# First stage of a two-block transformer kernel: TensorE sums the squares of x, the first loads and activation tables come in another order, and the first weight unit is split in four

## The chip, the cores and the metric

The kernel runs on one core of one Trainium2 chip. The metric is the device time of one execution in microseconds (us). It has five instruction streams: TensorE (PE in the rows, with its weight loads as PEld), VectorE (DVE), ScalarE (ACT), GpSimd (POOL) and SyncE (SP), which issues nearly all DMA transfers. A PE row with `f32` is fp32 or fp32r data of 4 bytes.

## The reference

x has 256 tokens of 1024 channels. The first block computes `h = rmsnorm(x, norm_mix_g)` and `p = h @ w_in`, and goes on from p to a sliding-window attention and an mLSTM, an output projection, a cross attention to `mem` and a feed-forward layer; a second block follows (gated delta rule, then stick-breaking attention). What matters here is the very first step:

```
def rmsnorm(x, g):
    y = x * rsqrt(mean(x * x, axis=-1) + 1e-6)
    return y * g
p = rmsnorm(x, norm_mix_g) @ w_in        # 1024 x 2824
```

Beside it `c_act = silu(c_2)`, a vector of 1024, is computed at the start and used by the second block's modulation matrices.

## The kernel before, in words

**Layout.** x lies transposed in SBUF: 8 chunks of 128 channels on the partitions, 256 tokens in the free dimension. It is loaded in four transfers x0 to x3 of two chunks each (256 KB). A weight matrix is cut into units of 1024 x 256 (1 MB); a unit is loaded into one of NRAW = 5 buffers `raw`, and split into two fp32r tiles: `whi` (a ScalarE copy, job `hi`) and `wlo = raw - whi` (VectorE, job `lo`), each in PIECES = 4 pieces of two chunks. A product of the two activations tiles `p0hi`, `p0lo` with them is three fp32r matmuls of 128x256 per 128 columns (line 1841), so a unit is 48 matmuls in four parts of 12.

**The order of work** is written by a planner, class `Plan`: it makes one list of jobs, and each engine runs its own jobs of this list in that order, waiting on semaphores. LAG = 1 means that the `lo` of a piece is put behind the `hi` of the next one. Nothing is reordered when the kernel runs.

**The first stage.** ScalarE waits for the vector table `vec` (192 KB, with gains and c), computes silu(c) (line 999), then squares each x pair (job `sq`, line 1032) into one of two buffers `tr`. VectorE adds the two halves and adds up the pairs (job `sqadd`, lines 1399 to 1404) into `acc`. TensorE multiplies `acc` with a matrix of ones in plain fp32 (job `ones`, line 1870), which sums over the partitions and leaves the sum in every row of PSUM bank `stats`. ScalarE loads the table set with ln and exp (line 994) and computes rs = exp(-0.5 ln(sum/1024 + eps)) (job `rs`, lines 1046 and 1048; it also waits for `con`, the first 264 columns of constants with the ones matrix and eps). Then the job list has the four `hi` pieces of the first weight unit with three of its `lo`, then the norm in five groups of 1, 1, 2, 2, 2 chunks (GROUPS): `xg` is x*gain*rs on VectorE (one instruction per chunk, line 1373), `ghi` the fp32r copy on ScalarE (line 1061), `glo` the remainder on VectorE (line 1376). Then `cr` (a constant, line 1445), and the products of the first unit, between which the pieces of the next unit are split.

**The DMA queue of SP** issues, in this order: vec, x0 to x3, con, weight units 0 to 2, conr, the rest of con, the two gate matrices g, units 3 and 4, mem; from unit 5 on it waits until the buffer's last `lo` is done.

`arrived(k)` is what a reader of unit k waits for: the semaphore of its buffer, which each load raises by 16. `stats_free()` makes TensorE wait until the last user of the bank `stats` has read it.

Of the kernel before, what the change touches and what calls it, by code (L numbers as in the profile page):

```python
# [14 lines left out]
T = 256  # L15
# [6 lines left out]
NRAW = 5  # L22
# [3 lines left out]
PIECES = 4  # L26
# [24 lines left out]
NCON0 = 8 + 2 * 128  # L51
# [97 lines left out]
def is_ada(unit):  # L149
# [4 lines left out]
COUNTED = {  # L154
    "hi": "hi", "lo": "lo", "unit": "unit", "adarow": "adarow", "adacp": "adacp", "adacol": "adacol",
    "adaadd": "adaadd",
    "sq": "sq", "sqadd": "sqadd", "ones": "ones", "rs": "rs",
    "xg": "norm_dve", "xm": "norm_dve", "xs": "norm_dve", "glo": "norm_dve", "fin": "norm_dve",
    "xa": "norm_act", "ghi": "norm_act",
    "aq": "proj_act", "ak": "proj_act", "cid": "proj_act", "csilu": "proj_act", "mo": "proj_act",  # L160
# [31 lines left out]
class Plan:  # L192
# [17 lines left out]
    def add(self, kind, *i):  # L210
        self.jobs.append((kind, *i))
        self.done.add((kind, *i))
# [158 lines left out]
    def make(self):  # L371
        add = self.add
        later = self.deferred.append
        add("csilu", "c")
        for i in range(4):
            self.stat("mix", i)
        self.rstd("mix")
        self.load_units()
        for _ in range(PIECES):
            self.prep_unit()  # L380
        for _ in self.gain_steps("mix"):
            pass
        add("cr")

        def on_mqk(i):
# [374 lines left out]
def program(nc, xT, memT, vec, con, conr, wg1, wg2, wst, wsd, outT):  # L760
# [11 lines left out]
    with ctx:  # L772
# [3 lines left out]
        def sem(name):  # L776
            return ctx.enter_context(nc.semaphore(name))

        S = {n: sem("s_" + n) for n in sorted(set(COUNTED.values()))}
        s_raw = [sem(f"s_raw{i}") for i in range(NRAW)]  # L780
        s_in = {n: sem("s_in_" + n) for n in ("x0", "x1", "x2", "x3", "mem", "vec", "con", "con2", "conr", "g")}
        s_out = sem("s_out")
# [2 lines left out]
        def on(*job):  # L785
            return S[COUNTED[job[0]]], rank[job]

        def tick(kind):
            return S[COUNTED[kind]], 1

        def landed(name):
            return s_in[name], 32 if name == "g" else 16

        def arrived(k):
            return s_raw[k % NRAW], 16 * (k // NRAW + 1)

        def at(name, i=0):
            return plan.at(name, i)
# [5 lines left out]
        raw = [sb(f"raw{i}", [P, 2048]) for i in range(NRAW)]  # L804
        whi = [sb(f"whi{i}", [P, 2048], F32R) for i in range(NHL)]
        wlo = [sb(f"wlo{i}", [P, 2048], F32R) for i in range(NHL)]
        cst = sb("cst", [P, NCON])
        crt = sb("crt", [P, NCONR], F32R)
        vc = sb("vc", [P, NVEC])
        x = sb("x", [P, KC, T])  # L810
# [12 lines left out]
        rs = sb("rs", [P, T])  # L823
# [43 lines left out]
        def V(name, i=0, n=1, p=P):  # L867
            a = VEC[name][0]
            return vc[0:p, a + i:a + i + n]
# [9 lines left out]
        ident, ones = C("ident"), C("ones")  # L879
# [56 lines left out]
        def sq_tile(site, i):  # L936
            if site == "mem":
                return flat(xk[:, 2 * i:2 * i + 2, :])
            return tr[4 + i % 2]

        stats = ps[7]
# [6 lines left out]
        @block.sync  # L948
        def _(e):
            def load(name, dst, src):  # L950
                e.dma_start(dst, src).then_inc(s_in[name], 16)

            na = nb = 0
            load("vec", vc[:, :], vec)
            for i in range(4):
                load(f"x{i}", x[:, 2 * i:2 * i + 2, :], xT[:, 2 * i:2 * i + 2, :])
            load("con", cst[:, 0:NCON0], con[:, 0:NCON0])
            for k, (name, i, kc, w) in enumerate(units):
                if k == 3:
                    load("conr", crf, conr)  # L960
                    load("con2", cst[:, NCON0:], con[:, NCON0:])
                    load("g", g1[:, :, :], wg1)
                    load("g", g2[:, :, :], wg2)
                if k == 5:
                    load("mem", m_x[:, :, :], memT)
                if kc == 8:
                    src = wst[na]
                    na += 1
                else:
                    src = wsd[nb]  # L970
                    nb += 1
                if k >= NRAW:
                    if is_ada(units[k - NRAW]):
                        e.wait_ge(*on("adarow", k - NRAW))
                    else:
                        e.wait_ge(*on("lo", k - NRAW, 3))
                e.dma_start(raw[k % NRAW][:, 0:kc * w], src).then_inc(s_raw[k % NRAW], 16)
            for i in range(4):
                e.wait_ge(*on("resb", i))
                e.dma_start(outT[:, 2 * i:2 * i + 2, :], x[:, 2 * i:2 * i + 2, :]).then_inc(s_out, 16)  # L980
            e.wait_ge(s_out, 64)
# [6 lines left out]
        def _(act):  # L988
            e, own = Once(act), Own(own_act)
# [7 lines left out]
            def silu(out, in_, f=ACT.Silu):  # L997
                table["lnexp"] = False
                return act.activation(out, in_, f)

            e.wait_ge(*landed("vec"))
            e.wait_ge(zeroed, 1)
            silu(cact[:, :, 0], V("c", 0, 8)).then_inc(*tick("csilu"))
            for kind, *i in jobs:
                if kind == "hi":
                    k, q = i
                    kc, w = units[k][2:]
                    per = -(-kc // PIECES)
                    a, b = q * per * w, min(kc, (q + 1) * per) * w
                    n = real[k] - 1  # L1010
                    e.wait_ge(*arrived(k))
                    if n >= NHL:
                        e.wait_ge(S["unit"], n - NHL + 1)
                    act.activation(whi[n % NHL][:, a:b], raw[k % NRAW][:, a:b], ACT.Copy).then_inc(*tick("hi"))  # L1014
                elif kind == "adacp":
                    k, = i
                    e.wait_ge(*on("adarow", k))
                    act.activation(arow[:, :], stats[:, T:2 * T], ACT.Copy).then_inc(*tick("adacp"))
                elif kind == "sq":
                    site, n = i  # L1020
# [6 lines left out]
                    else:  # L1027
                        e.wait_ge(*on("res", {"x": "wout", "ffn": "xo", "kv": "outa"}[site], n))
                    if n >= 2:
                        e.wait_ge(*on("sqadd", site, n - 2))  # L1030
                    src = NORM[site][0]
                    act.activation(sq_tile(site, n), flat(src[:, 2 * n:2 * n + 2, :]), ACT.Square).then_inc(*tick("sq"))  # L1032
                elif kind == "rs":
                    site, = i
                    e.wait_ge(*on("ones", site))
                    e.wait_ge(*landed("con"))
                    if site == "x":
                        e.wait_ge(*on("xg", "mem", 4))
# [10 lines left out]
                elif kind == "ghi":  # L1049
                    site, n = i  # L1050
# [11 lines left out]
                elif kind == "xa":  # L1062
                    site, n = i
# [3 lines left out]
                    for c in range(*GROUPS[n]):  # L1067
                        ins = act.activation(tmp[:, c, :], tmp[:, c, :], ACT.Identity, scale=mod[:, A + c:A + c + 1],  # L1068
                                             bias=mod[:, B + c:B + c + 1])
# [3 lines left out]
                elif kind == "aq":  # L1073
                    n, = i
# [5 lines left out]
                elif kind == "cid":  # L1080
                    n, = i
                    bank = bank_of("mqk", n)
                    e.wait_ge(*unit_done("mqk", n))
                    for m in range(2):
                        c = 2 * n + m
                        ins = act.activation(mqk[:, c, :], bank[:, m * T:(m + 1) * T], ACT.Identity,
                                             scale=V("cqk_w", c * 4 + 3), bias=V("cqk_b", c))
                    ins.then_inc(*tick("cid"))
                elif kind == "csilu" and i != ["c"]:
                    n, = i  # L1090
# [278 lines left out]
        def _(v):  # L1369
# [8 lines left out]
            for kind, *i in jobs:  # L1378
# [13 lines left out]
                elif kind == "sqadd":  # L1392
# [1 line left out]
                    s = sq_tile(site, n)  # L1394
                    e.wait_ge(*on("sq", site, n))
                    if n == 0:
                        if site != "mix":
                            e.wait_ge(*on("ones", {"mem": "mix", "x": "mem", "ffn": "x", "kv": "ffn"}[site]))
                        v.tensor_tensor(acc[:, :], s[:, 0:T], s[:, T:2 * T], ALU.add).then_inc(*tick("sqadd"))
                    else:  # L1400
                        own.mark(v.tensor_tensor(s[:, 0:T], s[:, 0:T], s[:, T:2 * T], ALU.add))
                        e.wait_ge(*own.last)
                        e.wait_ge(*on("sqadd", site, n - 1))
                        v.tensor_tensor(acc[:, :], acc[:, :], s[:, 0:T], ALU.add).then_inc(*tick("sqadd"))
# [398 lines left out]
        def _(t):  # L1803
# [8 lines left out]
            for kind, *i in jobs:  # L1812
# [51 lines left out]
                elif kind == "ones":  # L1864
# [3 lines left out]
                    stats_free()  # L1868
                    stat.append(("rs", site))
                    t.matmul(stats[:, 0:T], ones, acc[:, :], start=True, stop=True).then_inc(*tick("ones"))  # L1870
                elif kind == "f_ones":
                    e.wait_ge(*on("dacc", 7))
                    t.matmul(ps[3], ones, acc2[:, :], start=True, stop=True).then_inc(*tick("f_ones"))
# [375 lines left out]
```

## Time and profile before

| | |
|---|---|
| median of 3 runs | 995.97 us (995.44 to 1001.0) |
| the profiled execution | 992.34 us, of which span 990.6 us |
| TensorE busy (matmul) | 908.5 us, 92% of the span |
| VectorE, ScalarE busy | 601.1 us, 504.4 us |
| mean granted TensorE clock | 0.962 |
| moved by DMA | 148.25 MB, mean 150 GB/s |

The times in the rows are counted from the span's start. The profile was taken of one execution; its time is 3.6 us under the median of the others. TensorE's clock has two levels here, 2.4 GHz (a granted clock of 1.00) and 1.2 GHz (0.50). The chain of waits is the path that ended last, followed back from the last instruction; in its rows "issue" is time in which the engine waited for nothing that the profile shows.

### The profile page before, as it was taken

The numbers are of one execution on the slowest core, as the hardware profiler recorded it, in microseconds if no ns is written. First come the engines' busy times: TensorE is split into PE (matmuls) and PEld (weight loads), VectorE is DVE, ScalarE is ACT, GpSimd is POOL, SyncE is SP. The second block draws the span as 40 slices with busy tenths as digits, with TensorE's granted clock in tenths as the row PEclk, the third lists the DMA queues.
The fourth block names the chain that finished last, engine by engine and source line by source line (L and its number), as shares of the span: only waits on it lengthen the run. The fifth ranks groups of instructions, "written<-read, shape, count | busy, mean of one in ns | idle before, by whom it ended". The sixth has DMA issues, their size and how long they took to land.

```text
span 990.6 us, 16996 instructions
## 1 busy us (share of the span) xinstructions
PE 908.5 (92%) x7132; PEld 837.2 (85%) x7132; DVE 601.1 (61%) x1215; ACT 504.4 (51%) x1029; POOL 0.5 (0%) x5
## 2 busy tenths in 40 slices
PE   3979899999999999999969899989898879999998
PEld 3957698989899999999959687979797778988888
DVE  5378756675577777775656576666665465443345
ACT  5245554444445555555564625352644457456762
POOL 0000000000000000000000000000000000000000
PEclk9898999999999999999977899999999979999999
DMA  9423444563356676655652423223222134642211
GB/s 347 148 73 119 143 171 164 207 219 128 118 183 216 250 255 239 229 179 190 208 191 98 152 97 135 74 85 129 85 86 85 43 128 138 247 169 86 69 61 43
DMA packets 22541, 148.25 MB, mean 150 GB/s; under 512 B 2625, under 2 KB 3137, under 8 KB 6337
## 3 DMA queue, kind: packets, MB, share of 16 engines
q1 hardware_dynamic: 22464, 147.17, 41.6%
q8 instruction: 56, 0.92, 0.4%
q14 instruction: 21, 0.16, 0.0%
HBM read 146.11 MB, written 1.05 MB: 149 GB/s over the span
## 4 chain that ended last, share of the span: by engine, by line
PE 80%; DVE 11%; ACT 7%; issue 1%; DMA 1%; SPq 0%; DVEq 0%; ACTq 0%
PE ps L1841 55%; PE ps L1854 3%; PE ps L2073 2%; PE ps L2066 2%; DVE wlo L1376 2%; PE ps L2058 2%; PE ps L1884 1%; DVE kT L1373 1%; PE ps L1862 1%; ACT L994 1%; PE ps L2140 1%; DVE vt L1373 1%; ACT tmp L1068 1%; PE ps L2131 1%; PE ps L2004 1%
## 5 line engine op out<-in xcount | busy, mean ns | idle before, releaser
L1841 PE MATMUL ps<-p0hi,whi 128*128 128x256 f32 x1128 | 338.5, 300 | 16.9 <-DVE p0lo L1376 12.4
L1841 PE MATMUL ps<-p0lo,whi 128*128 128x256 f32 x1128 | 324.5, 288 | 0.0
L1841 PE MATMUL ps<-p0hi,wlo 128*128 128x256 f32 x1128 | 324.2, 287 | 0.0
L1376 DVE TENSOR_TENSOR wlo<-raw,whi 128x512 fp32r<-128x512 f32 (+2 forms) x436 | 272.8, 659 | 17.2 <-ACT whi L1014 15.4
L1841 PEld LDWEIGHTS ps<-p0hi,whi 128*128 128x128 f32 x1128 | 221.6, 196 | 34.4 <-issue 24.9
L1014 ACT ACTIVATE whi<-raw 128x512 fp32r<-128x512 f32 (+2 forms) x436 | 239.8, 600 | 8.3 <-DMA raw<-wst 8.2
L1841 PEld LDWEIGHTS ps<-p0lo,whi 128*128 128x128 f32 x1128 | 222.1, 197 | 0.7 <-issue 0.5
L1841 PEld LDWEIGHTS ps<-p0hi,wlo 128*128 128x128 f32 x1128 | 221.5, 196 | 0.0
L1841 PE MATMUL ps<-zhi,whi 128*128 128x256 f32 x176 | 49.3, 280 | 0.0
L1841 PE MATMUL ps<-zlo,whi 128*128 128x256 f32 x176 | 49.1, 279 | 0.0
L1841 PE MATMUL ps<-zhi,wlo 128*128 128x256 f32 x176 | 49.1, 279 | 0.0
L1841 PE MATMUL ps<-q1hi,whi 128*128 128x256 f32 x128 | 39.4, 308 | 3.3 <-DVE q1lo L1376 3.3
L1841 PE MATMUL ps<-q1lo,whi 128*128 128x256 f32 x128 | 37.6, 294 | 0.0
L1841 PE MATMUL ps<-q1hi,wlo 128*128 128x256 f32 x128 | 37.4, 292 | 0.0
L1854 PE MATMUL ps<-raw,cact 128*32 128x256 f32 x512 | 36.3, 404 | 0.0
L1391 DVE TENSOR_TENSOR mod<-ps,vc 128x2 f32<-128x2 f32 x32 | 5.0, 156 | 48.9 <-PE ps L1862 48.9
L1841 PEld LDWEIGHTS ps<-zhi,whi 128*128 128x128 f32 x176 | 33.1, 188 | 0.4 <-DVE tr L1511 0.4
L1841 PEld LDWEIGHTS ps<-zlo,whi 128*128 128x128 f32 x176 | 33.1, 188 | 0.0
L1841 PEld LDWEIGHTS ps<-zhi,wlo 128*128 128x128 f32 x176 | 33.1, 188 | 0.0
L1733 DVE TENSOR_TENSOR tmp<-ps,cst 128x512 f32<-128x512 f32 x24 | 16.5, 688 | 27.1 <-PE ps L2058 27.0
L1373 DVE SCALAR_TENSOR_TENSOR tr<-ps,tr 128x384 f32<-128x384 f32 (+1 forms) x21 | 11.6, 551 | 33.4 <-ACT tr L1356 29.0
L1032 ACT ACTIVATE tr<-x 128x512 f32<-128x512 f32 x16 | 10.1, 632 | 42.1 <-DVE x L1497 28.0
(338 smaller groups left out, 1589.6 us busy)
## 6 DMA issues: line engine op xcount, KB each, us to landing
raw<-wst SPq DMA_DIRECT2D x125, 1024.0 KB, 5.0
raw<-wsd SPq DMA_DIRECT2D x16, 704.0 KB, 4.8
x<-xT SPq DMA_DIRECT2D x4, 256.0 KB, 4.9
m_x<-memT SPq DMA_DIRECT2D x1, 1024.0 KB, 18.1
outT<-x SPq DMA_DIRECT2D x4, 256.0 KB, 2.3
cst<-con SPq DMA_DIRECT2D x1, 768.0 KB, 13.2
smo<-conr SPq DMA_DIRECT2D x1, 192.0 KB, 11.8
vc<-vec SPq DMA_DIRECT2D x1, 187.5 KB, 2.4
```

The source lines that it names most:

```text
L994: act.preload_act_table_set(LNEXP)
L1014: act.activation(whi[n % NHL][:, a:b], raw[k % NRAW][:, a:b], ACT.Copy).then_inc(*tick("hi"))
L1032: act.activation(sq_tile(site, n), flat(src[:, 2 * n:2 * n + 2, :]), ACT.Square).then_inc(*tick("sq"))
L1068: ins = act.activation(tmp[:, c, :], tmp[:, c, :], ACT.Identity, scale=mod[:, A + c:A + c + 1], bias=mod[:, B + c:B + c + 1])
L1373: return v.scalar_tensor_tensor(out=out, in0=a, scalar=s, in1=b, op0=op0, op1=op1)
L1376: return v.tensor_tensor(lo, src, hi.bitcast(F32), ALU.subtract)
L1733: v.tensor_tensor(Xm[n_ % 2][:, :, :], ps[4 + 2 * (n_ % 2)].rearrange("p (n t) -> p n t", n=4), rep(C("mlev", lev * P, (lev + 1) * P), 4), ...
L1841: ins = t.matmul(o, a, b, start=first and q == 0, stop=last and q == len(ops) - 1, skip_group_check=True)
L1854: ins = t.matmul(stats[g:g + 32, T:2 * T], cact[:, c, :], r[:, c * T:(c + 1) * T], start=c < 4, stop=c >= 4)
L2058: ins = t.matmul(ps[4 + 2 * (n_ % 2)][:, n * P:(n + 1) * P], Am[n_ % 2][:, n // 2, n % 2 * P:(n % 2 + 1) * P], Tm[n_ % 2][:, n, :], start= ...
L2066: ins = t.matmul(ps[4 + 2 * (n_ % 2)][:, n * P:(n + 1) * P], Um[n_ % 2][:, n, :], Xm[n_ % 2][:, n, :], start=True, stop=True)
L2073: ins = t.matmul(ps[3 + 2 * (n_ % 2)][:, n * P:(n + 1) * P], Xm[n_ % 2][:, n, :], Um[n_ % 2][:, n, :], start=True, stop=True)
```

## The change

Four things are changed, all of them before the first product:

- The sum of squares. The four `sqadd` and the `ones` of this norm are gone. In their place TensorE takes each squared pair as it comes (job `mones`): two plain fp32 matmuls of 128x256 with the ones matrix, eight in all, which add up in `stats`. A square buffer is now freed by the `mones` that read it. The other norms keep the old way.
- The first loads. `con` and `vec`, in this order, are issued by ScalarE's queue at its start and no longer by SP's. SP begins with x0.
- The tables. The ln/exp table set is loaded right behind silu(c), ahead of the first square.
- The first weight unit. It is loaded in four quarters of 512 columns (256 KB, rows of 2 KB), each with a semaphore of its own. Its `hi` and `lo` pieces no longer stand ahead of the norm but one each behind the norm's groups 1 to 4. The planner therefore gives VectorE this order: xg0, xg1, glo0, xg2, glo1, xg3, glo2, lo piece 0, xg4, glo3, lo piece 1, glo4, lo piece 2, cr, lo piece 3; before, lo pieces 0 to 2 stood in front of xg0 and lo piece 3 behind cr.

```diff
@@ class Plan, make
         add("csilu", "c")
         for i in range(4):
-            self.stat("mix", i)
-        self.rstd("mix")
+            add("sq", "mix", i)
+            add("mones", i)
+        add("rs", "mix")
         self.load_units()
-        for _ in range(PIECES):
-            self.prep_unit()
-        for _ in self.gain_steps("mix"):
-            pass
+        for step, _ in enumerate(self.gain_steps("mix")):
+            if step in (1, 2, 3, 4):
+                self.prep_unit()
         add("cr")
@@ arrived
-            return s_raw[k % NRAW], 16 * (k // NRAW + 1)
+            return s_raw[k % NRAW], 16 * (k // NRAW + (k % NRAW > 0))
@@ SP
             na = nb = 0
-            load("vec", vc[:, :], vec)
             for i in range(4):
                 load(f"x{i}", x[:, 2 * i:2 * i + 2, :], xT[:, 2 * i:2 * i + 2, :])
-            load("con", cst[:, 0:NCON0], con[:, 0:NCON0])
...
-                e.dma_start(raw[k % NRAW][:, 0:kc * w], src).then_inc(s_raw[k % NRAW], 16)
+                if k == 0:
+                    for q in range(4):
+                        e.dma_start(raw[0][:, q * 512:(q + 1) * 512], src[:, q * 512:(q + 1) * 512]).then_inc(s_first[q], 16)
+                else:
+                    e.dma_start(raw[k % NRAW][:, 0:kc * w], src).then_inc(s_raw[k % NRAW], 16)
@@ ScalarE
+            act.dma_start(cst[:, 0:NCON0], con[:, 0:NCON0]).then_inc(s_in["con"], 16)
+            act.dma_start(vc[:, :], vec).then_inc(s_in["vec"], 16)
             e.wait_ge(*landed("vec"))
             e.wait_ge(zeroed, 1)
             silu(cact[:, :, 0], V("c", 0, 8)).then_inc(*tick("csilu"))
+            lnexp()
...
-                    e.wait_ge(*arrived(k))
+                    if k:
+                        e.wait_ge(*arrived(k))
+                    else:
+                        e.wait_ge(s_first[q], 16)
...
                     if n >= 2:
-                        e.wait_ge(*on("sqadd", site, n - 2))
+                        e.wait_ge(*(on("mones", n - 2) if site == "mix" else on("sqadd", site, n - 2)))
...
-                    e.wait_ge(*on("ones", site))
+                    e.wait_ge(*(on("mones", 3) if site == "mix" else on("ones", site)))
@@ TensorE
+                elif kind == "mones":
+                    n, = i
+                    e.wait_ge(*on("sq", "mix", n))
+                    e.wait_ge(*landed("con"))
+                    for c in range(2):
+                        ins = t.matmul(stats[:, 0:T], ones, sq_tile("mix", n)[:, c * T:(c + 1) * T], start=n + c == 0, stop=n + c == 4)
+                    ins.then_inc(*tick("mones"))
+                    if n == 3:
+                        stat.append(("rs", "mix"))
```

## Rows read from the trace of the kernel before

**Rows 1.** The page, part 4, shares of the chain that ended last.

```profile
PE 80%; DVE 11%; ACT 7%; issue 1%; DMA 1%; SPq 0%; DVEq 0%; ACTq 0%
```

**Rows 2.** Chain of waits, 0 to 20 us: start us, us, what.

```profile
2.57 6.19 DMA x<-xT
8.78 0.64 ACT tr L1032
9.44 0.44 DVE tr L1401
9.90 0.44 DVE acc L1404
10.38 1.23 PE ps L1870 x2
11.63 1.28 ACT L994
12.92 0.48 ACT rs L1046
13.43 0.42 ACT rs L1048
...
17.74 2.26 PE ps L1841 x9
```

**Rows 3.** Timeline of VectorE: start us, us, operation, idle before it.

```profile
14.40 1.89 DVE L1376 TENSOR_TENSOR wlo<-raw,whi 128x512 fp32r<-128x512 f32 x3 [4.07 <-ACT whi L1014]
16.21 0.87 DVE L1373 SCALAR_TENSOR_TENSOR tmp<-x,vc,rs 128x256 f32<-128x256 f32 x2
...
20.03 0.87 DVE L1373 SCALAR_TENSOR_TENSOR tmp<-x,vc,rs 128x256 f32<-128x256 f32 x2
```

**Rows 4.** Timeline of the queue of SP and of ScalarE at the start.

```profile
0.73 0.37 SPq L951 DMA_DIRECT2D vc<-vec  x1
...
1.12 1.28 ACT L999 ACT_TABLE_LOAD   x1 [1.12 <-POOL cact L985]
3.15 0.22 ACT L999 ACTIVATE cact<-vc 128x8 f32<-128x8 f32 x1 [0.75 <-DMA vc<-vec]
```

**Rows 5.** DMA issues of the first 60 us: KB each, median us from issue to landing.

```profile
cst<-con SPq DMA_DIRECT2D x1, 132.0 KB, 6.1
vc<-vec SPq DMA_DIRECT2D x1, 187.5 KB, 2.4
```

**Rows 6.** Stretches of 5 and 1 us: busy per engine; last columns PEclk, DMA share, GB/s.

```profile
0.00:5.00 5.00, 0.00 (x0) 0.00 (x0) 0.00 (x0) 1.50 (x2) 0.51 (x5) 1.00 0.48 140
5.00:6.00 1.00, 0.00 (x0) 0.00 (x0) 0.15 (x1) 0.78 (x2) 0.00 (x0) 1.00 0.89 270
```

**Rows 7.** Line 1870 from 10 to 12.5 us: duration ns min/median/max, start us, form.

```profile
L1870 PE MATMUL ps<-acc,cst x2: 634/714/793, 10.4 to 11.0; 128*128 128x256 f32 x2
```

**Rows 8.** Eight fp32 matmul records of 128x256 in the chain of waits.

```profile
250.25 1.73 PE ps L1985 x8
```

**Rows 9.** Timeline of TensorE where the spacing of the first unit's products changes.

```profile
21.72 0.38 PE L1841 MATMUL ps<-p0hi,whi 128*128 128x256 f32 x1
...
21.93 0.28 PE L1841 MATMUL ps<-p0lo,whi 128*128 128x256 f32 x1
...
22.05 0.28 PE L1841 MATMUL ps<-p0hi,wlo 128*128 128x256 f32 x1
```

**Rows 10.** Split of the first weight pieces, VectorE: duration ns min/median/max.

```profile
L1376 DVE TENSOR_TENSOR wlo<-raw,whi x8: 682/684/691, 14.4 to 24.9; 128x512 fp32r<-128x512 f32 x8
```

**Rows 11.** Stretches of 1 us behind a gap of TensorE, columns as in rows 6.

```profile
220.00:221.00 1.00, 0.00 (x0) 0.00 (x0) 0.91 (x2) 1.00 (x3) 0.00 (x0) 1.00 0.00 0
...
223.00:224.00 1.00, 1.00 (x8) 1.00 (x8) 1.00 (x3) 1.00 (x3) 0.00 (x0) 0.65 0.00 0
...
226.00:227.00 1.00, 1.00 (x8) 1.00 (x7) 0.64 (x2) 0.00 (x0) 0.00 (x0) 0.64 0.85 352
```

**Rows 12.** The longest piece of the chain of waits from 10 to 50 us.

```profile
17.74 21.76 PE ps L1841 x168
```

More of the change, by code:

```diff
@@ L156 @@
     "adaadd": "adaadd",
-    "sq": "sq", "sqadd": "sqadd", "ones": "ones", "rs": "rs",
+    "sq": "sq", "sqadd": "sqadd", "ones": "ones", "mones": "ones", "rs": "rs",
     "xg": "norm_dve", "xm": "norm_dve", "xs": "norm_dve", "glo": "norm_dve", "fin": "norm_dve",
@@ L779, in program @@
         S = {n: sem("s_" + n) for n in sorted(set(COUNTED.values()))}
+        s_first = [sem(f"s_first{q}") for q in range(4)]
         s_raw = [sem(f"s_raw{i}") for i in range(NRAW)]
@@ L1396, in _ @@
                     if n == 0:
-                        if site != "mix":
-                            e.wait_ge(*on("ones", {"mem": "mix", "x": "mem", "ffn": "x", "kv": "ffn"}[site]))
+                        if site != "mem":
+                            e.wait_ge(*on("ones", {"x": "mem", "ffn": "x", "kv": "ffn"}[site]))
                         v.tensor_tensor(acc[:, :], s[:, 0:T], s[:, T:2 * T], ALU.add).then_inc(*tick("sqadd"))
```

## Prediction, on record before the change was run

> **What bounds the kernel now.** I read the page first: four fifths of the chain that ended last are TensorE work [rows 1], so time is won only where TensorE stands still or runs at its low clock. Then the chain at the start, because the whole change lies ahead of the first product. It shows a latency chain [rows 2]: the last pair x3 lands at 8.76 (2.57 + 6.19), its square ends at 9.42, two adds, the ones matmul to 11.61, the table load of 1.28, Ln and Exp until 13.85, and the first product only at 17.74. From there 168 product records follow without a gap to 39.50 [rows 12]: the first units are fed well enough once they have begun. So the change is worth, in first order, the distance by which 17.74 moves. The timeline of VectorE shows why rs at 13.85 does not yet start the norm: three weight pieces stand in front, and xg0 begins at 16.21 [rows 3]. From xg0 to the product are 17.74 - 16.21 = 1.53.
>
> The sum is made against the profiled execution, 992.34 us. The median of the three runs is 995.97, 3.6 above it; I add my difference to that median.
>
> **The change, part by part.**
>
> *Loads.* SP's first issue took 0.37 and the next came 0.43 later (0.73 to 1.16 in the same timeline; the first start is in [rows 4]). Without vec in front, x0 to x3 go out 0.43 earlier. But con (132 KB) now competes with x instead of following it: at the 270 GB/s of the stretch from 5 to 6 [rows 6] it costs x3 some 0.5. x3 then lands at about 8.76 - 0.43 + 0.5 = 8.8, unchanged. Three more issues on SP for the quarters delay units 1 and 2 by about 1.3, three times 0.43; no one waits for them: unit 0 is not wanted before its first `hi`, which comes after rs, and unit 1 only after unit 0's four pieces. I cost the quarters at nothing; the cover is the whole chain to rs.
>
> *vec.* Here it turns. vec was first and landed 2.4 after its issue [rows 5]; silu(c) ran at 3.15, long before x0 [rows 4]. Now it is the second transfer of another queue. Bounds: 2.4 after an issue at about 1.2, so 3.6, if the second queue has a free way; con's 6.1 [rows 5] after 1.2, so 7.3, if it fares as the transfer that stood behind x. In between: con, vec and the half of x that is served beside them are 0.83 MB. Before, 0.70 MB were moved by 5.0 (140 GB/s over 5 us) and 0.83 by 5.5 [rows 6]; 0.43 earlier is 5.1, and 0.5 from the last byte to the semaphore (vec before: 192 KB moved, landed at 3.13) makes 5.6. I take **5.6**, with 3.6 and 7.3 as ends.
>
> *Tables.* Before, silu's table load ran at 1.12 while vec was on its way. The second load, 1.28 [rows 2], leaves the place between the ones matmul and Ln and stands between silu (0.22, [rows 4]) and the first square. With vec at 5.6: silu to 5.84, load to 7.13, first square to 7.78. Before, the first square ended at about 5.8. Its saving of 1.28 at the end is real only if TensorE is not the one that comes last.
>
> The trace shows a load of 1.28 with Ln 0.01 behind it [rows 2]. The Trainium skill ("ScalarE: Activation LUTs", What ACT_TABLE_LOAD costs) counts about 1.38 more for a drain with each switch of sets. The rows here show no such piece; by the page the first square would end 1.4 later, and my result would be 998.9.
>
> *TensorE sums the squares.* This is the costly part. Before, one fp32 matmul of 256 columns: two records, 793 and 634 ns, 1.23 together [rows 7, 2]; the second began 0.43 after the first (11.60 - 0.79 = 10.81 against 10.38). At the high level eight records took 1.73 [rows 8], 0.216 each, so a matmul is 0.43 at the high level and 0.85 at the low one, plus 0.37 after the last one is streamed (1.23 - 0.85). Eight matmuls are **6.8 at the low level**, 3.5 at the high one. TensorE has done nothing before, and begins at the low level: the first unit's products are spaced 0.21 until 21.93 and 0.12 after it [rows 9], although the page's column says 1.00; the rise came 4.2 after the first product. In its place went seven adds of VectorE, of which two (0.92) were on the path.
>
> So first matmul at 7.83, rise 4.2 later at 12.0; by then 4.2 of 6.8 are done, the other 2.6 take 1.3 at the high level, and with 0.3 behind the last the sum stands at **13.6**. The squares of x2 and x3 wait for the matmuls of x0 and x1 (two buffers), but TensorE always has the next pair by then; it is TensorE that comes last, not x3: 8.8 + 0.63 + one pair (1.71 + 0.37) would be 11.5. Before, Ln began at 12.92; now at 13.65. rs at 13.65 + 0.93 = 14.58 (12.92 to 13.85 before), **0.7 later**.
>
> *Norm and weight pieces.* xg0 follows rs at once, at 14.6: this wins 16.21 - 13.85 = 2.36. But the first product now needs lo piece 0, and that stands behind xg0, xg1, glo0, xg2, glo1, xg3, glo2 in VectorE's order. Before, xg0 to the end of glo2 went from 16.21 to 20.03 [rows 3], 3.82; with lo piece 0, 0.68 [rows 10], and 0.14 to the product it is 4.64 instead of 1.53, **3.11 lost**. Net of this part: 0.75 lost. ScalarE's pieces fit between its norm copies and are not last. First product: 14.58 + 0.03 + 4.64 = **19.2**, against 17.74: **1.5 later**.
>
> *After it.* The rest of VectorE's work was only reordered. Behind lo piece 0 come 0.87 + 0.69 + 0.68, so part 1 has its piece 2.2 after the first product; part 0 takes 12 x 0.214 = 2.6 at the low level. No wait, and a margin of 0.4. TensorE has idled 5.6 since the ones and begins low again, as before. All that follows is shifted.
>
> Sum: +0.7 + 0.8 = +1.5: 992.34 + 1.5 = 993.8 for a profile, and 995.97 + 1.5 = **997.5** for the median. This is no change by measurement: about 1% (10 us) can be told from none.
>
> **Rivals.**
>
> *A, TensorE is not last.* vec lands at 3.6 (first square ends at 5.8, as before) and the clock rises after 3 us. Then 3.0 of 6.8 are done at 8.9, the rest would end at 10.8, and x3's pair binds: 9.4 + 0.05 + 0.85 + 0.3 = 10.6. Either way about 10.8; Ln at 10.85, rs 11.8, first product 16.5: **-1.3, 994.7**. For it: ScalarE's queue is empty. Against it: the DMA engines' share was 0.89 in the stretch from 5 to 6 [rows 6]. The Trainium skill ("DMA: Bandwidth & Descriptors", Issuing engines are not separate DMA queues) speaks against this rival and against the change: transfers issued by several engines share the same 16 DMA engines, and only issue time is saved. Chance 0.2.
>
> *B, slower than forecast.* vec lands at 7.3 and the clock does not rise in the sum: first matmul at 9.5, sum at 9.5 + 6.8 + 0.4 = 16.7, rs 17.7, first product 22.3: **+4.6, 1000.6**. It decides from a vec later than about 6.5. Chance 0.15.
>
> *C, the clock outlives the gap.* The eight matmuls raise the clock and the products start high. Then a unit is bound by VectorE instead: 2.2 for part 0, then three parts of 1.44, 6.5 against 19 x 0.214 + 29 x 0.12 = 7.5 before: 1.0 back, **+0.5, 996.5**. Against it: TensorE stood 2.13 at 220 and the clock fell at 223.3, rising again near 226.6, though it worked from 222 on [rows 11]; here the gap is 5.6. The Trainium skill ("TensorE: Matmul & The Clock Gate", HAM oscillation) says the same of gaps between bursts. Chance 0.1.
>
> *D, clearly slower.* A shift of a few us moves later stretches against the falls of the clock. A fall as at 223.3 to 226.6 [rows 11] costs half its 3.3, 1.7; it takes six more of them for 10 us, **1006**. Place: the late stages with gaps on TensorE. Chance 0.03; the mirror image, **986**, 0.02.
>
> That the change does nothing at all is one more case: quarters and SP order surely do nothing, but the sum on TensorE cannot be idle.
>
> **How the numbers follow.** Forecast (+0.3 to +3) 0.5; A 0.2, B 0.15, C 0.1, D and its mirror 0.05. Predicted 997.5. The range reaches from A with a margin of 1.5 for the scatter of runs (995.44 to 1001.0 before), 993.2, to B, 1000.8. A, B, C and the forecast all lie within 1%: same 0.95, slower 0.03, faster 0.02.
>
> **What would show it.** Right: eight fp32 matmuls (16 records) ending near 13.6, table load between silu and the first square at about 6, the first square after 7, xg0 right behind Exp, a product near 19.2 spaced 0.21 at first, nothing of the quarters in any wait. Wrong: the sum ending before 11 (A), after 15.5 (B), the first products spaced 0.12 (C), or a first product near the old time with a total that differs by more than 3 us, which then comes from elsewhere.

## The result, and the profile after

The changed kernel takes 1004.17 us (median of 7 executions, 996.65 to 1004.83), the kernel before, beside it, 995.44 (7 executions, 988.89 to 1001.0). The ratio is 1.0085, 95% interval 1.0045 to 1.0126: slower. The forecast was 997.5 and its range ended at 1000.8. The difference is under 1%, but its interval does not reach 1.

Two more series, on two chips, gave 1.0071 (1.0044 to 1.0097) and 1.0026 (0.9998 to 1.0055), with means 4.9 and 3.1 above the kernel before beside them. Ahead of the first of the two I had expected 3 to 4 if only the delay of the first product is lasting, and 7 to 9 if something of the change makes the clock fall more often; it came between. Over all 31 executions of the change the mean is 1001.2, over 116 of the kernel before 995.9: the lasting loss is **5.3 us**, smaller than the first median says. (Errors given here and below are standard errors of the difference of two means; this one is 0.7.)

One execution of the kernel before at 1077.1, with a granted clock of 0.794, is a slow run and left out everywhere, while four of the 116, at 1002.5 to 1003.3, are also over 1.5% above their fastest but have the clock of their neighbours (0.949 to 0.951) and are kept: without them the loss is 5.6.

The profiled execution took 1004.83, with a span of 1003.0 against 990.6.

Below, the head is the time from the start to the first product. The chain of waits of the changed kernel from 0 to 22 us (start us, us, what), to be read beside [rows 2]:

```profile
1.17 5.74 DMA vc<-vec
...
6.94 0.22 ACT cact L1002
...
7.17 1.28 ACT L997
...
8.46 0.64 ACT tr L1041
...
9.15 6.15 PE ps L1885 x16
...
15.32 0.48 ACT rs L1055
...
15.83 0.42 ACT rs L1057
...
16.28 0.49 DVE tmp L1382
...
19.59 0.60 DVE p0lo L1385
20.19 0.61 DVE wlo L1385
...
20.85 1.22 PE ps L1850 x4
```

The chain no longer begins with x but with vec, which lands at 6.91. Then silu, the table load and one square follow each other, and the sixteen records of the sum (line 1885; two records for each of the eight matmuls) take 6.15 until 15.30. rs is ready 2.4 later than before (16.25 against 13.85), and the norm begins at once behind it. From xg0 to the first product are 4.57, against 1.53 before. The first product comes at 20.85, **3.1 later** than the 17.74 of before.

The two transfers of ScalarE's queue, from the DMA issues of the first 4 us (KB each, us to landing), against 6.1 and 2.4 in [rows 5]:

```profile
vc<-vec ACTq DMA_DIRECT2D x1, 187.5 KB, 5.7
cst<-con ACTq DMA_DIRECT2D x1, 132.0 KB, 4.1
```

The head is 3.1 of the 12.4 us by which the spans differ. Where the rest is, three stretches tell. First the kernel before, then the changed one (busy per engine, then PEclk, DMA share, GB/s):

```profile
550.00:580.00 30.00, 25.94 (x176) 22.19 (x175) 15.54 (x32) 16.74 (x36) 0.00 (x0) 0.89 0.34 133
...
700.00:730.00 30.00, 27.12 (x207) 24.25 (x204) 19.23 (x37) 16.67 (x32) 0.00 (x0) 1.00 0.29 106
...
770.00:800.00 30.00, 26.88 (x202) 25.75 (x203) 17.79 (x34) 13.36 (x25) 0.00 (x0) 0.94 0.23 75
```

```profile
550.00:580.00 30.00, 25.68 (x149) 20.24 (x142) 15.78 (x33) 15.53 (x32) 0.00 (x0) 0.77 0.38 141
...
700.00:730.00 30.00, 27.30 (x188) 23.58 (x187) 16.17 (x30) 19.26 (x35) 0.00 (x0) 0.90 0.27 95
...
770.00:800.00 30.00, 24.61 (x140) 21.49 (x139) 12.49 (x24) 11.15 (x21) 0.00 (x0) 0.72 0.10 36
```

Nearly the same work (in the second trace it stands 3 to 13 us later) meets more of the low clock: 0.77, 0.90 and 0.72 instead of 0.89, 1.00 and 0.94. With VectorE's instructions of both traces matched by form and order, the changed kernel is 3.2 behind at 40 us, 4.4 from 110, 2.9 from 230 to 550, 6.0 from 560, 9.1 from 720 and 12.8 from 780. Each step is a stretch in which the clock stands low in one profile and high in the other. The one step back, 1.5 at 223, is the fall at 223.3 to 226.7 that the kernel before has [rows 11] and the changed one has not. Nothing there was edited. The mean granted clock is 0.947 against 0.962, which is 106 us at the low level against 75 (twice the missing share, times the span).

### The profile page after: what moved, and what is told of

Its sections match the earlier page's. It is cut to its first block, busy times and chain, and to the rows that moved or that the text cites. A ratio compares the mean times of both kernels' runs of the same rounds, so it can differ in the third digit from the quotient of the medians.

```text
span 1003.0 us, 17016 instructions
## 1 busy us (share of the span) xinstructions
PE 921.4 (92%) x7146; PEld 848.0 (85%) x7146; DVE 598.4 (60%) x1208; ACT 504.4 (50%) x1029; POOL 0.5 (0%) x5
## 4 chain that ended last, share of the span: by engine, by line
PE 79%; DVE 11%; ACT 7%; issue 1%; DMA 1%; ACTq 0%; DVEq 0%
PE ps L1850 54%; PE ps L1863 3%; PE ps L2091 2%; PE ps L2084 2%; PE ps L2076 2%; DVE wlo L1385 2%; PE ps L1902 1%; PE ps L1871 1%; DVE kT L1382 1%; ACT L997 1%; PE ps L2158 1%; DVE vt L1382 1%; ACT tmp L1077 1%; PE ps L2149 1%; PE ps L2022 1%
## 5 line engine op out<-in xcount | busy, mean ns | idle before, releaser
L1385 DVE TENSOR_TENSOR wlo<-raw,whi 128x512 fp32r<-128x512 f32 (+2 forms) x436 | 273.2, 660 | 14.2 <-ACT whi L1023 12.5
```

Source lines behind the costliest of these rows:

```text
L1385: return v.tensor_tensor(lo, src, hi.bitcast(F32), ALU.subtract)
```

## The experiments

**The stand of the clock.** By this I mean where the rises and falls of the clock lie against the work. For each profile I read when the clock first falls after the first product. In the kernel before that is within the gate matmuls, 32 of 8 columns each (line 1884), which run from 39.50 to 43.46. In the kernel before and then in the changed one:

```profile
42.00:43.00 1.00, 1.00 (x9) 1.00 (x8) 0.00 (x0) 0.00 (x0) 0.00 (x0) 0.70 0.00 0
```

```profile
44.00:45.00 1.00, 1.00 (x10) 1.00 (x10) 0.00 (x0) 0.00 (x0) 0.00 (x0) 0.90 0.07 16
```

A mean of 0.70 over 1 us at levels of 1.00 and 0.50 puts the fall at 42.40, that is 24.66 after the first product (17.74); a mean of 0.90 puts it at 44.80, 23.95 after 20.85. The table has this distance for every profile, and the rest of the span behind the first product:

| first fall less first product | rest of the span | profile of |
|---|---|---|
| 23.35, 23.43, 23.47, 23.60, 23.69 | 975.0, 974.8, 975.1, 975.3, 975.1 | early matmuls, delay ahead, pieces first, change again, best |
| 23.95, 24.08 | 982.1, 982.5 | the change (above, and beside the delays) |
| 24.23, 24.23, 24.23, 24.35 | 982.3, 975.5, 975.6, 975.6 | delay behind (twice), vec before con, VectorE sum |
| 24.66, 24.82, 24.85 | 972.9, 972.7, 972.8 | before, best with whole unit, before + delay |
| 25.04 | 976.8 | before + early table |
| 26.40, 26.47 | 974.3, 977.8 | vec first, change + longer delay |

Kernels that differ in the edits below, with nearly the same distance, agree within 0.5 us (first row) and 0.2 (fourth), and one kernel at two distances (the change) differs by 7. So what follows the head is the same work in all of them, and its time goes with where the clock's changes stand against it. The first fall alone does not settle it: at 24.23 one kernel, the delay behind, has both 982.3 and 975.5, and the two of the last row, 0.07 apart, differ by 3.5. These may be edges between two courses of the clock; nothing here tested that. The stand differs from execution to execution, and with it the time of the unchanged kernel, 987.4 to 1003.3.

**Early TensorE work alone**, on no path: the kernel before with

```diff
+            e.wait_ge(*landed("x0"))
+            for _ in range(5):
+                t.matmul(ps[6][:, 0:T], x[:, 0, 0:P], x[:, 1, :], start=True, stop=True)
```

> The kernel before, with five plain fp32 matmuls of 128x256 on x0 that no one reads, on TensorE from 5.2 to about 9.5, ahead of the ones matmul. They are on no path. Theory: time and first product (17.7) as before, within 1 us in the mean. Rival (early work of TensorE changes where or how often the clock falls later): mean 3 us or more above before, with more stretches at the low clock in the trace.

First product at 17.57, mean of 12 executions 995.9 beside 995.7 of before; ratio 1.0009 (0.9984 to 1.0034). The matmuls from 4.81 to 9.44 cost nothing that can be told from zero. The test is weaker than it looks: their ten records took 4.63, as the low level gives for ten (0.43 each, and 0.37 behind the last), and the trace records no rise before 20.45. So it says that early work at the low clock is not the cause; it does not test early work that raises the clock, as the sum does.

**A pure delay** in the kernel before, ahead of its last addition of the squares:

```diff
+                        if site == "mix" and n == 3:
+                            for _ in range(4):
+                                own.mark(v.tensor_tensor(flat(tmp[:, 0:2, :]), s[:, :], s[:, :], ALU.add))
+                                e.wait_ge(*own.last)
```

> The kernel before, with four additions of 128x512 that no one needs on VectorE ahead of the last addition of the squares: a pure delay of 2.9 us on the chain, first product near 20.6, nothing else changed. Theory (the loss behind the head is only the stand of the later stages against the clock's falls, which are tied to the program's start): the total is 8 to 9 us above before, like the change. Rival (the falls of the clock stand differently in every execution, so a shift costs itself alone): 2.9 above before, 998.5, with the scatter of before.

First product at 20.53; ratio 1.0029 (0.9997 to 1.0061), mean 997.8 against 995.8: the delay of 2.8 costs 2.0 with an error of 1.3. A shift nearly as large as the change's costs itself, as far as that error tells. The theory, that any shift would cost 8 to 9, is refuted; the falls are not tied to the program's start: the first stood at 45.38 instead of 42.40, 24.85 behind the product instead of 24.66.

**vec first**, con alone on ScalarE's queue:

```diff
+            load("vec", vc[:, :], vec)
             for i in range(4):
                 load(f"x{i}", ...)
...
-            act.dma_start(vc[:, :], vec).then_inc(s_in["vec"], 16)
```

> The change, with vec back at the head of SP's queue and con alone on ScalarE's. Theory (vec's landing starts the late sum, TensorE's eight matmuls bound it): vec lands near 3.2, first square ends near 5.9 on x0, the eight fp32 matmuls end near 12.0, first product near 17.6 instead of 20.85. Rival (the eight matmuls are the cost whatever starts them, or con is late): sum ends after 14, first product after 19.5. For the total: if the loss behind the head (5.6 of 8.7 us) comes from where the later stages stand against the falls of the clock, it goes with the head and the total is that of before within 2 us; if the loss is from something else that the change leaves in the kernel, 1000 or more remain.

Its chain from 0 to 22 us:

```profile
0.73 2.89 DMA vc<-vec
...
5.86 5.57 PE ps L1885 x16
...
16.98 5.06 PE ps L1850 x22
```

vec lands at 3.62, the sum begins 3.3 earlier than in the change and still takes 5.57, and the first product comes at 16.98, 3.9 earlier than in the change and 0.8 earlier than before. The head is as expected; the total is not: ratio 1.0026 (0.9998 to 1.0054), mean 998.9 against 995.8. That is neither the total of before within 2 nor the 1000 or more of the rival: a head better than before's goes with a total 3.1 above it, with an error of 1.2.

**The sum on VectorE** as before, loads, tables and pieces of the change (the diff shows the order of jobs; the waits go with it):

```diff
-            add("sq", "mix", i)
-            add("mones", i)
-        add("rs", "mix")
+            self.stat("mix", i)
+        self.rstd("mix")
```

> The change, with the squares summed on VectorE and one ones matmul as before; loads, tables and weight pieces as in the change. Theory: vec still lands near 6.9, squares end near 10.8, adds 0.9, matmul 1.23, rs near 13.9, first product near 18.5, that is 2.3 earlier than the change and 0.8 later than before. Rival (vec alone is the cost): first product stays above 20. Rival on the clock: the eight early matmuls are what puts the later falls of the clock elsewhere; then the total falls by clearly more than 2.3.

```profile
1.18 5.44 DMA vc<-vec
...
11.45 0.44 DVE acc L1412
...
11.93 1.24 PE ps L1878 x2
...
13.19 0.48 ACT rs L1054
...
18.71 3.36 PE ps L1849 x14
```

The sum ends at 13.17 though vec is late (6.62), 2.1 ahead of the sum on TensorE, or 1.8 if the 0.3 by which vec was earlier is taken off. Ratio 1.0023 (0.9995 to 1.005), mean 998.1: 2.3 above before, with an error of 1.3, for a first product 1.0 later.

**The four pieces ahead of the norm**, as before, the rest of the change:

```diff
-        for step, _ in enumerate(self.gain_steps("mix")):
-            if step in (1, 2, 3, 4):
-                self.prep_unit()
+        for _ in range(PIECES):
+            self.prep_unit()
+        for _ in self.gain_steps("mix"):
+            pass
```

> The change, with the four weight pieces ahead of the norm as before; sum on TensorE, loads and tables as in the change. Theory: rs stays at 16.25, first product 3.9 behind it near 20.15, 0.7 earlier than the change: the interleaving itself loses 0.7. Rival (the interleaving gains, as it lets the norm start 2.4 earlier): first product 21.5 or later. Total: 0.7 less than the change if the clock's falls stay where they are; up to 6 less if a shift of 0.7 brings the later stages elsewhere against them.

```profile
8.92 5.35 PE ps L1886 x16
...
17.66 0.41 DVE tmp L1383
...
19.11 2.90 PE ps L1851 x12
```

rs was ready at 15.21, the first product 3.90 behind it; in the change it was 4.60 behind. So the interleaving loses 0.70. Ratio 1.0034 (1.001 to 1.0059), mean 999.3: 3.4 above before, with an error of 1.0, for a first product 1.4 later.

**The table load alone**, in the kernel before: `lnexp()` behind silu(c).

> The kernel before, with the ln/exp table loaded right behind silu(c); nothing else changed. Theory: the load ends near 4.7, before x0 is there, so it is hidden; Ln starts 1.28 earlier near 11.65 and the first product comes near 16.5; mean of the total 1.3 under before. Rival by the Trainium skill (ScalarE: Activation LUTs, What ACT_TABLE_LOAD costs, with about 1.38 of drain at each switch): the first square would start near 6.1 instead of 5.2, and a gap would stand behind the load.

```profile
10.46 1.24 PE ps L1871 x2
11.72 0.48 ACT rs L1047
...
16.54 3.54 PE ps L1842 x15
```

Ln follows the ones matmul at once; the first product is 1.2 earlier and the mean 993.7 against 995.7 (ratio 0.998, 0.9954 to 1.0006). Of the 1.38 of drain that the Trainium skill names (ScalarE: Activation LUTs, What ACT_TABLE_LOAD costs) no run here shows anything: in the change silu begins at 6.94 for 0.22, the load at 7.17, the square at 8.46.

**vec before con**, both on ScalarE's queue, the rest of the change:

> The change, with vec issued ahead of con on ScalarE's queue. Theory (vec is late because con's transfer stands in front of it and x's packets are served beside it): vec lands between 3.5 and 4.8 instead of 6.0 to 6.9, con between 4.5 and 6.5, and the sum begins at 6.3 or so, first product near 17.9. Rival (a transfer on ScalarE's queue is slow in itself beside SP's): vec lands after 5.5.

```profile
0.73 4.13 DMA vc<-vec
...
7.10 6.43 PE ps L1885 x16
...
19.07 5.98 PE ps L1850 x34
```

vec lands at 4.86: con in front of it made 1.2 to 2.0 of its lateness. Another 1.2 go when vec stands at the head of SP's queue, ahead of x (3.62); whether x beside it or ScalarE's queue made these, no run here separates. The first product is later than expected because the sum began at 7.1, not 6.3, and took 6.43. The one execution took 996.51.

**Does the sum on TensorE tie the first product to the clock?** The change, vec first and pieces first, all with the sum on TensorE, had totals above what their heads explain, by 2.6, 3.9 and 2.1. The sum's length goes with the clock's rise in it: 5.32 to 6.43 in ten profiles. In the trace the rise is seen in the weight loads of the sum (shortest, median and longest in ns; the change, then the delay behind): 338 at the low level, 190 at the high one, and more of them short where the rise comes early.

```profile
L1885 PEld LDWEIGHTS ps<-tr,cst x16: 190/338/338, 9.1 to 14.7; 128*128 128x128 f32 x16
```

```profile
L1889 PEld LDWEIGHTS ps<-tr,cst x16: 186/229/337, 8.4 to 13.1; 128*128 128x128 f32 x16
```

The clock's record in the trace begins with this rise, at 14.07 in the change, 4.9 behind the start of the sum; over the ten profiles it comes 2.9 (sum 5.32) to 5.5 (sum 6.43) behind the start. A rise that is 2.6 later ends the sum 1.1 later. So the first product follows the rise: it came 6.5 to 7.7 behind it in the seven profiles without a delay between. The theory is that its distance to the clock's later changes therefore takes only a part of the values that it takes in the kernel before. In the table six of these seven stand at 23.43 to 24.23 and one at 26.40, none with a rest under 974.3; of the seven profiles without that sum five stand at 24.35 to 25.04, three of them with the best rest, 972.7 to 972.9. Delays test it. In the change, between rs and xg0 (1.9 us, and with two more additions 3.4):

```diff
+                    if site == "mix" and n == 0:
+                        for w in (2, 2, 1):
+                            own.mark(v.tensor_tensor(flat(tmp[:, 0:w, :]), flat(x[:, 0:w, :]), flat(x[:, 0:w, :]), ALU.add))
+                            e.wait_ge(*own.last)
```

> The change, with three additions that no one needs on VectorE between rs and xg0: a pure delay of 1.9 us ahead of the first product. Theory: the sum on TensorE ends sooner or later with the moment at which the clock rises in it, so it ties the first product to the clock's changes, and ties it where the later stages meet more falls; a delay behind the sum moves the product off that place. Then the mean falls in spite of the delay, from the change's 1001.5 (19 executions) to 997 to 999, with executions under 995, which the change does not have. Rival (the excess of 3 us over the head is the change's own in some other way, or is chance): the delay adds itself, mean 1003.4.

> The change, with five such additions, a delay of 3.4 us. Theory: the first product stands against the clock's changes as in the change again, so the mean is the change's plus 3.4, near 1005, some 6 to 8 above the kernel with the delay of 1.9 though only 1.5 more was put in. Rival: 1.5 above that kernel.

With 1.9: ratio 1.0059 (1.0038 to 1.0081), mean of 8 executions 999.3. With 3.4: 1.0111 (1.0078 to 1.0143), mean of 6 executions 1004.7. The second is 5.4 above the first for 1.5 more delay, with an error of 1.5 (6 to 8 expected). The executions under 995 that I expected of the first did not come (lowest 996.61), and before was at 993.9 on this chip, so against before the first delay saved less than thought. Therefore a second test, on one chip: the same delay behind the sum, one of 2.0 ahead of it (three squares that are overwritten), and the change.

```diff
+                    if site == "mix" and n == 0:
+                        for _ in range(3):
+                            own.mark(act.activation(sq_tile(site, n), flat(src[:, 0:2, :]), ACT.Square))
+                            e.wait_ge(*own.last)
```

> The change, with three squares of x0 that are overwritten, on ScalarE ahead of its first square: a delay of 2.0 us ahead of the sum on TensorE. Theory (the sum ties the first product to the rise of the clock within it): a delay ahead of the sum leaves that tie as it is, so it costs its full 2.0: mean 2.0 above the change on the same chip. Rival (any delay moves the product off the bad place, or the excess is chance): the same as with a delay of 1.9 behind the sum.

> The change with a delay of 1.9 us between rs and xg0, once more, beside the one ahead of the sum. Theory: the mean is 2 to 3 below the kernel with the delay ahead, and not above the change. Rival: equal to the delay ahead within 1, and 1.9 above the change.

> The change itself, on the same chip as the two delays, as their base: mean 5 to 7 above before, no execution under 996.

Chains of the delay ahead, then of the delay behind:

```profile
10.32 5.71 PE ps L1889 x16
...
21.57 3.47 PE ps L1854 x16
```

```profile
8.41 5.32 PE ps L1889 x16
...
21.19 3.94 PE ps L1854 x17
```

| on one chip | first product | ratio to before (95%) | mean | lowest |
|---|---|---|---|---|
| before | 17.7 | | 997.7 (27) | 990.42 |
| the change | 20.70 | 1.0026 (0.9998 to 1.0055) | 1000.8 (12) | 995.99 |
| delay behind the sum | 21.19 | 1.0028 (0.9997 to 1.0058) | 1000.5 (12) | 994.60 |
| delay ahead of the sum | 21.57 | 1.0074 (1.0042 to 1.0106) | 1004.4 (10) | 998.10 |

(The first product of before is that of its profile, taken elsewhere.) The delay behind the sum cost -0.3 with an error of 1.3; the one ahead of it 3.6, with an error of 1.4. That is the order that the theory asks for (3.9 apart with an error of 1.5, 2 to 3 expected); the rival wanted them equal, which lies 2.7 errors away. The change was 3.1 above before here, less than the 5 to 7 that I expected, with one execution just under 996.

The granted clocks of the single executions say the same without the length of the head. The time at the low level is twice the missing share times the span. In kernels with the sum on TensorE a part of it is the low stretch between the sum and the first unit (17.5 to 24.3 in the change's profile), which the other traces do not record, as theirs begin with the rise in the first unit; the third column has it from the profiles, one for each kernel (three of the change, two of the delay of 1.9).

| kernel (executions) | at the low level, mean us (error) | of it ahead of the first unit's rise | rest |
|---|---|---|---|
| before (109 with a clock on record) | 86 (1) | | 86 |
| before + delay, best, early table, VectorE sum (12 each) | 84, 86, 86, 89 (2 to 3) | | 84 to 89 |
| early matmuls (12) | 93 (3) | | 93 |
| the change (31) | 99 (2) | 5.7 | 93 |
| vec first, pieces first (12 each) | 100, 97 (3, 2) | 6.8, 3.4 | 94, 94 |
| delay ahead of the sum (10) | 103 (3) | 3.4 | 100 |
| delay of 1.9 behind the sum (20) | 93 (2) | 6.8 | 87 |
| delay of 3.4 behind the sum (6) | 103 (3) | 10.2 | 93 |

With the sum on TensorE there are some 7 us more at the low level behind the head than before (14 with the delay ahead), with the short delay behind the sum there are not, and with the longer one there are again. The early matmuls fit less well: 93 without a longer time. Over the single executions 1 us at the low level goes with 0.37 us of time in the kernel before and 0.32 in the change, so the change's 7 us are an estimated 2.4 us of time.

**A better version**: vec first, con on ScalarE's queue, early table, squares summed on VectorE, quarters, and two pieces ahead of rs (the diff shows the order of jobs only):

```diff
         for i in range(4):
             self.stat("mix", i)
+        self.prep_unit()
+        self.prep_unit()
         self.rstd("mix")
...
-            if step in (1, 2, 3, 4):
+            if step in (2, 3):
```

> What the steps point to: vec first on SP, con on ScalarE's queue, ln/exp table right behind silu(c), squares summed on VectorE with one ones matmul, quarters for the first unit, and two of its four pieces split ahead of rs, while ScalarE and VectorE wait, the other two between the norm groups. Theory: squares end near 9.3, ones matmul near 11.6, rs near 12.6 (1.28 less), first product 1.5 behind it near 14.1, 3.6 earlier than before; mean of the total 3 to 4 under before. Rival (the quarters land too late for the pieces ahead of rs, or the products run out of pieces): first product after 15.5 or gaps of TensorE between 14 and 24, total within 1.5 of before.

Chain from 8 to 16 us, and ScalarE's and VectorE's timelines where the pieces are split:

```profile
10.40 1.24 PE ps L1880 x2
...
11.66 0.48 ACT rs L1056
...
12.61 0.49 DVE tmp L1383
...
14.15 2.05 PE ps L1851 x8
```

```profile
9.27 1.27 ACT L1024 ACTIVATE whi<-raw 128x512 fp32r<-128x512 f32 x2
```

```profile
10.26 1.29 DVE L1386 TENSOR_TENSOR wlo<-raw,whi 128x512 fp32r<-128x512 f32 x2
```

Both pieces lie in the time in which ScalarE and VectorE waited for the ones matmul. First product at 14.15, 3.6 earlier than before; median 990.87 against 995.73, mean 991.8 against 995.7, ratio **0.9967** (0.9937 to 0.9997). It beats the change, 1000.7 beside it, clearly, and the kernel before by 3.9 with an error of 1.2, about the 3.6 of its head.

The same with the unit loaded whole:

> The version with vec first, the sum on VectorE and two pieces ahead of rs, with the first unit loaded whole instead of in quarters. Theory (quarters are worth something only where pieces stand ahead of rs): the unit lands near 11.4, Ln stands behind the two pieces on ScalarE and begins near 12.6 instead of 11.66, first product near 15.1 instead of 14.15. Rival (quarters do nothing here either): first product within 0.3 of 14.15.

```profile
3.06 8.75 DMA raw<-wst
...
12.98 0.37 ACT rs L1055
...
15.36 9.70 PE ps L1850 x63
```

The unit lands at 11.81, Ln waits behind the pieces, and the first product comes 1.2 later. The quarters are worth that here, and nothing in the change, where the first piece is split at 17.51. Its single total (989.87) says nothing on this: its clock stood well (24.82 in the table).

## Why the prediction failed, step by step

- **Loads, vec: mis-sized.** vec was put at 5.6 with ends of 3.6 and 7.3; it landed at 6.91, and at 6.0 to 6.7 in the change's other profiles. The transfer in the second queue came between a free way and the place behind x, as written, but nearer to the latter. That is past the 6.5 from which rival B was to decide; B's other condition, no rise of the clock in the sum, did not come.
- **Tables: right in the sum, not in its sentence.** The load stood in full (1.28) between silu and the first square. It was also gone in full behind the sum, where Ln began 0.02 after it though TensorE came last: the two cancel. The sentence that its saving is real only if TensorE is not last was wrong; the sum of the forecast did not use it. In the kernel before, moved alone, where vec is early, it gives 1.2.
- **The sum on TensorE: right in mechanism, 5.8 forecast, 6.15 measured** (5.32 to 6.43 over ten profiles, as the clock rises earlier or later in it; the rise was put 4.2 behind the start and came 4.9 behind it). Summed on VectorE it ends some 1.8 earlier with the same loads. Rival A fell: TensorE came last even with vec at 3.62.
- **Norm and pieces: right.** 4.57 from xg0 to the first product (4.64 forecast), a net loss of 0.70 by the experiment (0.75 forecast).
- **Quarters: right**, nothing.
- The head is thus +3.1 in the profile (+1.9 and +3.0 in two others) for a forecast of +1.5; 1.3 of the difference is vec's, 0.4 the sum's. By the head alone the median would have been about 999, inside the range.
- **"All that follows is shifted": wrong.** This step failed. In the profile 9.3 of 12.4 us arose later, where the work meets the clock. I had this mechanism as rival D, as a rare pile-up of six more falls at 1.7 each with a chance of 0.03. It needs no such pile-up: the profile has 14 falls where that of before has 12, but 31 us more at the low level, because several last longer (from 775.2 to 792.3 against 772.9 to 776.3). And it is common: the rest of one and the same kernel is 975 or 982 by where the clock stands. Two things follow. First, one profile and three times could not carry a range with 1.5 us of scatter at its lower end and 0.2 at its upper one (1000.6 of rival B to 1000.8): the kernel before itself runs from 987.4 to 1003.3, and 1001.0 was already among the three. Second, the forecast took the change as neutral to this, and it is not: its sum on TensorE lasts longer when the clock rises later. None of its 31 executions came under 995.99, while 31 of the 116 of before came under 993.3, which is that less a head of 2.7.
- What is shown: that the remainder goes with the stand of the clock, that a plain delay in the kernel before costs about itself, that early TensorE work at the low clock costs nothing measurable, and that a delay behind the sum costs less than one ahead of it. That the tie to the clock's rise is what removes the good cases is the theory that these fit, and it is argued: its intervals are wide (the two delays' ratios overlap between 1.0042 and 1.0058), and a sum that ties the product to the rise was not separated from any other work that raises the clock early. The 2.6 us between the lasting loss (5.3) and the head (2.7) are about the 2.4 estimated from the time at the low level. That the 9.3 of the profile and the 8.7 between the first two medians are larger is luck: the profiled execution was one of the long ones (rest 982), and the median of seven held some 3 us of chance.

## What to carry to other kernels

Work put on TensorE before it has been busy is paid, at first, at its low clock: eight plain fp32 matmuls took 5.3 to 6.4 us here where seven additions on VectorE, hidden but for two, and one matmul did the same. A transfer that gates the start belongs ahead of the large ones and of one that nobody needs first: vec landed at 3.6 there, at 6.9 behind con and beside x. Fill the engines' wait for a reduction with work that does not need its result (here two weight pieces), and only then split a load so that this work can begin.

Where one kernel spreads over 1.6% with the clock, as this one, a dozen executions or more are needed before a difference under 1% means anything. A change ahead of the first product is better read in the trace: the head of the change was 1.9, 3.0 and 3.1 longer than before in its three profiles, while its times ran over 9 us.

## What the runs showed of the hardware

- One program on one core, on at least four chips: 987.4 to 1003.3 us, and the time goes with the mean granted clock. In the change's executions 0.955 to 0.957 goes with 995.99 to 998.55, and 0.946 to 0.951 with 1000.0 to 1004.99.
- The clock's column reads 1.00 from the start, in the change until 17 us, though the products of before are spaced as at the low level until 21.93 [rows 9]: it knows changes only from the first recorded one, here at 14.07 and before at 21.92. The rows of the changed kernel:

```profile
16.00:17.00 1.00, 0.00 (x0) 0.00 (x0) 0.72 (x2) 0.45 (x2) 0.00 (x0) 1.00 1.09 416
17.00:18.00 1.00, 0.00 (x0) 0.00 (x0) 0.91 (x4) 1.00 (x3) 0.00 (x0) 0.74 1.04 417
18.00:19.00 1.00, 0.00 (x0) 0.00 (x0) 1.00 (x4) 0.63 (x2) 0.00 (x0) 0.50 1.03 422
24.00:25.00 1.00, 1.00 (x9) 1.00 (x9) 1.00 (x3) 0.85 (x2) 0.00 (x0) 0.84 0.40 164
```

  It had risen within the sum, fell at 17.5 in the gap behind it and rose again at 24.3, so the products of the first unit began low in spite of the early work: rival C fell.
- vec took 2.9 us from issue to landing at the head of SP's queue, 4.1 at the head of ScalarE's beside x, and 4.8 to 5.7 behind con.
